# Order of experts, router table, fillers and bias products in a one-core mixture-of-experts step

## What is computed

```python
logits = (x2 @ w_router) + b_router            # 336 x 32
top_v, top_i = lax.top_k(logits, 4)
gates = jax.nn.softmax(top_v, axis=-1)
...
gu = xb @ w_gu[e] + b_gu[e]                    # D_MODEL 1024 -> 2 * D_FF 2048
gate = jnp.minimum(gu[:, :D_FF], 7.0)
up = jnp.clip(gu[:, D_FF:], -7.0, 7.0)
hid = (up + 1.0) * gate * jax.nn.sigmoid(1.702 * gate)
return hid @ w_dn[e] + b_dn[e]                 # 1024 -> 1024
```

## Time and profile before

| what | value |
|---|---|
| median of the runs | 1793.83 us |
| the profiled execution, its own time | 1794.13 us |
| its span | 1792.3 us |
| TensorE (PE) busy | 1596.8 us, 89% |
| VectorE / ScalarE / GpSimd busy | 363.6 / 372.3 / 122.1 us |
| share of the last chain: arrival of gate/up weights | 16% |
| DMA | 477.36 MB, 266 GB/s over the span |
| a free block of the loop: token turn / bias products / hidden turn | 0.71 / 1.09 / 0.66 us |
| the same: one piece of 4 products (8 instructions) | 1.72 us |
| the same: start of the token turn to start of the bias products | 0.94 us |

### The profile page before, as it was taken

One profiled execution on the slowest core, in us unless ns is written; L12 is line 12 of the kernel. 1 busy time (PEld: TensorE's weight loads), 2 busy tenths in 40 slices (PEclk: granted clock), 3 DMA queues, 4 the chain that ended last, 5 costly groups with the idle time before them and its releaser, 6 DMA issues.

```text
span 1792.3 us, 20636 instructions
## 1 busy us (share of the span) xinstructions
PE 1596.8 (89%) x7124; PEld 732.7 (41%) x7125; DVE 363.6 (20%) x859; ACT 372.3 (21%) x724; POOL 122.1 (7%) x219
## 2 busy tenths in 40 slices
PE   6899999999999997988879998878899978899894
PEld 4565665666666643322223332222233322233231
DVE  3443442223231123110101101100111100111015
ACT  3443242353430020110101111101111101111111
POOL 0100000000000000100001010100011100011000
PEclk9989999899999997998989999989899989899997
DMA  7212112221209524899998999999999999849898
GB/s 251 69 47 74 47 48 94 72 71 47 95 1 303 187 99 175 347 409 413 413 405 324 401 354 413 411 409 407 362 363 360 405 409 406 351 179 406 339 403 283
DMA packets 108777, 477.36 MB, mean 266 GB/s; under 512 B 12995, under 2 KB 16944, under 8 KB 75970
## 3 DMA queue, kind: packets, MB, share of 16 engines
q1 hardware_dynamic: 100696, 461.77, 65.9%
q0 software_dynamic: 7808, 15.00, 2.5%
q10 hardware_dynamic: 234, 0.08, 0.0%
HBM read 471.26 MB, written 15.50 MB: 272 GB/s over the span
## 4 chain that ended last, share of the span: by engine, by line
PE 70%; DMA 17%; DVE 5%; issue 3%; SPq 2%; ACT 1%; DVEq 0%; ACTq 0%; POOL 0%; POOLq 0%
PE bank L592 30%; PE bank L975 20%; DMA ring<-in_w_gate_up 16%; PE bank L998 16%; PE bank L596 3%; PE bank L981 1%; DVE r_kv L1346 1%; DVE r_v L1349 1%; DMA b_router_b<-in_b_router 1%; SPq L546 0%; SPq L553 0%; SPq L462 0%; DVE r_c L1349 0%; DVE r_qk L1343 0%; DVE ring L1343 0%
## 5 line engine op out<-in xcount | busy, mean ns | idle before, releaser
L975 PE MATMUL bank<-ring,r_kv 128*64 128x512 f32 x2184 | 521.1, 625 | 95.6 <-DMA ring<-in_w_gate_up 95.6
L975 PEld LDWEIGHTS bank<-ring,r_kv 128*64 128x64 f32 x2184 | 157.1, 142 | 408.7 <-issue 309.0
L998 PE MATMUL bank<-ring,r_kv 128*64 128x512 f32 x1248 | 294.6, 616 | 0.7 <-ACT r_kv L1063 0.7
L592 PE MATMUL bank<-r_xt,ring 128*128 128x336 f32 x848 | 256.6, 458 | 1.8 <-DVE r_xt L1346 1.5
L1343 DVE TENSOR_SCALAR r_kv<-bank 128x512 f32<-128x512 f32 (+1 forms) x80 | 54.9, 687 | 930.5 <-PE bank L981 924.0
L592 PEld LDWEIGHTS bank<-r_xt,ring 128*128 128x128 f32 x848 | 161.7, 194 | 83.4 <-issue 13.2
L998 PEld LDWEIGHTS bank<-ring,r_kv 128*64 128x64 f32 x1248 | 93.8, 145 | 200.6 <-issue 199.7
L1063 ACT ACTIVATE r_xt<-bank 128x512 f32<-128x512 f32 x39 | 23.3, 597 | 521.6 <-PE bank L998 521.6
L592 PE MATMUL bank<-ring 128*128 128x336 f32 (+4 forms) x336 | 98.2, 435 | 4.1 <-DVE ring L1502 3.9
L1289 ACT ACTIVATE r_o<-r_kv 128x512 f32<-128x512 f32 x39 | 24.6, 632 | 324.7 <-DVE r_kv L1343 324.7
L596 PEld LDWEIGHTS bank<-const,r_v 64*128 64x128 f32 (+3 forms) x524 | 45.4, 139 | 79.4 <-DVE r_v L1349 44.5
(11 more groups left out here) (235 smaller groups left out, 988.2 us busy)
## 6 DMA issues: line engine op xcount, KB each, us to landing
ring<-in_w_gate_up SPq DMA_DIRECT2D x256, 1024.0 KB, 17.1
ring<-in_w_down SPq DMA_DIRECT2D x128, 1024.0 KB, 14.6
ring<-in_w_in SPq DMA_DIRECT2D x12, 2048.0 KB, 8.1
ring<-in_w_proj_b SPq DMA_DIRECT2D x2, 2048.0 KB, 8.8
ring<-in_w_proj_a SPq DMA_DIRECT2D x2, 2048.0 KB, 8.9
ring<-in_w_out SPq DMA_DIRECT2D x2, 2048.0 KB, 7.8
ring<-y_rows SPq DMA_DIRECT2D x8, 512.0 KB, 9.1
ring<-in_w_uq SPq DMA_DIRECT2D x2, 1152.0 KB, 9.0
```

The lines of the kernel that those rows point to most:

```text
L592: ins = pe.matmul(out, l, r, start=(n == 0), stop=(n == len(pairs) - 1), **kw)
L975: ins = pe.matmul(half(gate_bank if q < 2 else up_bank, q % 2), xg[:, k, :], w[:, 512 * q:512 * q + 512], start=False, stop=False, skip_gr ...
L998: ins = pe.matmul(half(out_bank, t), hidT[:, j, BLK * h:BLK * h + BLK], w[:, h, 512 * t:512 * t + 512], start=(j == 0 and h == 0), stop=(j ...
```

## The change

- Experts are set apart by rank. VectorE makes for each expert a key (blocks x 32, and the expert's number for ties; expert 0 gets the lowest), its rank by key, and a place for each rank from a table of constants (`rank_at`, the bit-reversed number plus 4; expert 0 stays at place 0). With the counts above the order is 0, 21, 11, 31, **26**, 12, 2, 22, **20**, 16, 6, 27, **10**, 14, 4, 24, 1, 19, 9, 30, **8**, 13, 3, 23, **29**, 17, 7, 28, **18**, 15, 5, 25 (bold: more than one block). Two more products, "ord" and "st", bring blocks and first blocks in that order to all partitions; "pend" goes. SyncE reads the expert of a place from `experti` and loads its weights; `be` holds a block's expert for the biases, `bei` its place.
- One slot table. `spread` has 55 columns in place of 110, the table product writes both halves of the partitions with the same values (24 products of 55 columns), and the token row is worked out from the output row by rounding. GpSimd's part of `spread`, `valc` and "tab2" go.
- Fillers: products of 128x512 that nobody reads, 2 ahead of the turn of tile 2, 2 ahead of "ord", 5 ahead of "tab", 1 ahead of the first turn of tokens.
- Down biases: all 6 products stand within block 0's gate/up pieces, 4 ahead of piece 2 and 2 ahead of piece 5; the loop waits for all six adds.
- In the loop: ScalarE takes the sigmoid straight from the gate bank; VectorE works out min(sigmoid, its value at 7) x (up + 1), then min(gate, 7) x that, the gate read from its bank (the 1 is now added to the up biases once, ahead of the router stage). The two bias products of the up bank stand ahead of the turn of the hidden rows, the two of the gate bank behind it. `down(0)` and `down(1)` stand ahead of `gate_up(0, e1)`.

```diff
+def keep_going(b, n):
+    for _ in range(n):
+        pe.matmul(b[:, :], ident, const[:, 0:512], start=True, stop=True, skip_group_check=True)
...
+            keep_going(begin("x2T", 2, 0), 2)
             x2_turned(2)
...
-            pe.wait_ge(nblkT_set, 1)
-            b = begin("pend")
-            end(group(b[0:NE, 0:1], [(cst("below")[0:NE, 0:NE], nblkT[:, :])]), "pend")
+            keep_going(begin("ord"), 2)
+            pe.wait_ge(order_set, 1)
+            b = begin("ord")
+            end(group(b[:, 0:2 * NE], [(cst("ones")[0:NE, :], ordered[:, :])]), "ord")
+            pe.wait_ge(diag_set, 1)
+            b = begin("st")
+            end(group(b[:, 0:NE], [(cst("ones")[0:NE, :], diag[:, :])]), "st")
+            keep_going(begin("tab"), 5)
...
             for k in range(8):
+                if k == 2:
+                    for n in range(4):
+                        down_bias(banks[4 + n], n // 2, n % 2).then_inc(bd_full, 1)
+                if k == 5:
+                    pe.wait_ge(bd_free, 2)
+                    for n in range(4, 6):
+                        down_bias(banks[n], n // 2, n % 2).then_inc(bd_full, 1)
                 gate_up(k, 0)
...
-                bias(b + 1)
+                bias(b + 1, (2, 3))
                 hidden_turned(b)
-                pe.wait_ge(m_xg, b + 2)
-                gate_up(0, e1)
+                bias(b + 1, (0, 1))
                 pe.wait_ge(m_hidT, b + 1)
                 pe.wait_ge(yrow_free, b + 1)
+                pe.wait_ge(m_xg, b + 2)
                 down(0, e)
                 down(1, e)
+                gate_up(0, e1)
                 down(2, e)
                 gate_up(1, e1)
                 down(3, e)
...
-                act.wait_ge(m_gt, b + 1)
-                act.activation(sg, gt, ACT.Sigmoid, scale=ALPHA).then_inc(m_sig, 1)
+                act.wait_ge(m_gate, b + 1)
+                act.activation(sg, banks[2][:, :], ACT.Sigmoid, scale=ALPHA).then_inc(m_sig, 1)
...
-            signal(dve.tensor_reduce(nblkT, cmp6[0:NE, 0, :], AX.X, ALU.add), nblkT_set, 1)
...
+            step(stt(key, nblk[0:NE, :], float(NE), cst("key", NE)[:, 0:NE], ALU.mult, ALU.add))
+            step(ts(above, key, keyT, ALU.is_gt))
+            step(dve.tensor_reduce(rankT, above, AX.X, ALU.add))
...
+                x = sp.value_load(experti[0:1, bass.ds(e, 1)].bitcast(I32), min_val=0, max_val=NE - 1)
...
-                ts(gt, banks[2][:, :], LIMIT, ALU.min).then_inc(m_gt, 1)
...
-                ts(up, banks[3][:, :], LIMIT, ALU.min, -LIMIT, ALU.max).then_inc(m_read, 1)
+                ts(up, banks[3][:, :], LIMIT + 1.0, ALU.min, 1.0 - LIMIT, ALU.max).then_inc(m_read, 1)
...
-                tt(gt, gt, sg, ALU.mult).then_inc(m_dve, 1)
+                stt(glu, sg, SIG_LIMIT, up, ALU.min, ALU.mult).then_inc(m_dve, 1)
...
-                stt(hid, up, 1.0, gt, ALU.add, ALU.mult).then_inc(m_hid, 1)
+                stt(hid, banks[2][:, :], LIMIT, glu, ALU.min, ALU.mult).then_inc(m_hid, 1)
...
-            pool.tensor_tensor(spread[:, :, 0:NB1], inblk, valc.unsqueeze(2).broadcast_to([128, 12, NB1]), ALU.mult
-                               ).then_inc(tab_p, 1)
```

159 lines of the change are left out of this document (91 added, 68 removed).

## The result

The change takes 1783.98 us (median of 5 runs, 1779.22 to 1789.16), the kernel before 1793.83 us beside it (5 runs, 1791.90 to 1794.33): ratio 0.9948, 95% interval 0.9926 to 0.9971. That is 9.85 us less, where I had forecast 20.6 less. The direction and the range held, the size did not. The profiled execution of the change took 1789.16 us, the slowest of its five, with a span of 1787.3 us where 1792.3 stood; the experiments contain a second execution of the same kernel (a_again) with a span of 1781.7.

A forecast was written before the change was run, and what follows sets the result against it. TensorE was taken as bound by its own work plus 17 stalls on expert weight loads. Loop -15.7, block 1 -1.0, router stage -0.5 and block 0 -3.4 sum to -20.6: 1794.13 becomes 1773.5 us, range 1762 to 1784 (chance 0.72).

The forecast's parts named there:

- The model of the stalls: Loop waits for gate/up weights: from the third transition after a full ring; 96.1 us for 138.0, a gain of 41.9.
- the 17 places named: Expert places forecast to stall in the loop: 3, 4, 7, 8, 11, 12, 15 to 20, 23, 24, 27, 28, 31.
- Spacing alone: Loop: reordering experts by rank, without the other loop changes, was forecast to be worth about 0.
- 24.29: Forecast length in us of a loop block that finds its weights, where 23.60 us stood.
- Two bias products (0.55 us) now fill part of that hole: Behind the hidden rows' turn: a pair costed at 0.55 us in a 0.69 us idle, next product 0.69 us later.
- +26.2 us: Loop: cost of longer free blocks, 38 times 0.69 us, if nothing hid it.
- block 1: Loop's first block: 1.4 us of slow clock goes with the idle ahead of it, forecast -1.0 us.
- second rival: Loop: the clock falls at every turn, each block pays 2.5 to 3 us, about 1807 us; chance 0.05.
- router stage and block 0: Ahead of the loop: forecast -0.5 us for the router stage and -3.4 us for block 0.
- Block 0: First turn to first loop bias: 26.4 us becomes 23.0, -3.4 us (-4.4 to -1.7), with down biases inside the product.
- The stage ahead of it: Router stage: longer table path against earlier token turn and fillers holding the clock; -0.5 us, from -2 to +4.
- the signs I had named: Signs include free blocks 24.3 us, idle about 70 us, first loop bias at 715 to 718, clock above 0.5 from 676 to 690.

The follow-up runs named there:

- e5: The change with all four bias products ahead of the turn again and VectorE's old chain, down pieces still first; run twice, 1782.74 us in one, 0.9939 to 0.9952 of before.
- e8: The change with all four bias products behind the turn of the hidden rows; free block 24.8 us where the clock stays up, kernel time not given in the text.
- e9: The loop with four biases ahead of the turn and down pieces first, keeping only the two fillers before tile 2's turn; within 0.9939 to 0.9952 of before.
- e6: Four biases ahead of the turn, down pieces first, and the next block's token turn moved behind the hidden rows' turn; 0.9994 of before.
- e1: The change with experts left in the order of their numbers; 0.9998 of before.
- e3: The change with the old loop and experts by number, keeping the router table, fillers and down biases; loop 1010.8 us, kernel time not given in the text.
- e2: The change with TensorE's and VectorE's old loop, experts still spaced; loop 1007.5 us, against before slower, if at all, by 0.14%.
- e4: The change without any filler product; 0.9974 of before (0.9956 to 0.9991).
- e7: The change with four of six down bias products replacing the filler ahead of the first token turn; 1785.17 us, 0.9944 of before.
- e10: Token turn behind the hidden rows' turn, with TensorE's wait for turned tokens moved two down pieces later; 0.9942 of before.

## Why the prediction went wrong

**What held.** The model of the stalls: idle times at the 17 places named, ten of them long, and a short idle in the last block. Spacing alone was worth 3 us in the loop, near the 0 of the forecast, but cost 7 us at the end, which the forecast hadn't followed. The measured excess over free blocks is 90.0 us, 6.7 of it in the slow blocks, so 83.3 in stalls, where the forecast had 96.1: the longer free blocks gave the loads more time. The idle time is 56.1 us, where I had named about 70. e5 is the fair test of that model, since its free block (24.4 us) is nearly the one I had costed (24.29): its loop is 15.1 and 15.9 us shorter than before's, where the forecast had 17.4 for 37 blocks, or some 12 if each is 0.14 us longer; and its 93.5 and 92.7 us above 37 free blocks are close to the 96.1.

**The step that failed** is "Two bias products (0.55 us) now fill part of that hole; the next product still starts 0.69 us later than before", and so the term **+26.2 us**. I had halved the 1.09 us of the row of four. But the row itself says that these products have 32 rows each: the four stand in the four groups of rows of the array and run beside each other. The pair takes 1.07 us and outlasts the hole that it was to fill. The pages of both kernels show it in TensorE's busy time for the same number of bias products, before and in the change:

```profile
L965 PE MATMUL bank<-bgu,r_qk 32*64 32x512 f32 x312 | 44.2, 636 | 12.0 <-DVE r_kv L1343 12.0
```

```profile
L983 PE MATMUL bank<-bgu,r_qk 32*64 32x512 f32 x312 | 86.4, 643 | 5.5 <-DVE r_kv L1367 5.3
```

The Trainium skill ("TensorE: Matmul & The Clock Gate", the part on packing small matmuls) states just this, that products in different row groups overlap and together take about as long as one; the traces of the change and of e8 agree (two in 1.07, four in 1.09 us), and I hadn't laid it beside the row. That is 0.17 us of the 0.44 by which a free block is longer than forecast: the down product starts 1.59 us after the turn in the change and 1.42 in e5, with the hole bare. Another 0.14 us is the bare hole itself, 0.83 us later than before in e5 (1.42 for 0.59) and not the 0.69 read off the last block. The last 0.13 us is VectorE: its product now depends on the clip just before it. I had costed that chain at 0 by its durations, which held (0.69 us each, also the one that reads the bank); what I had not costed is the gap between dependent operations, 0.79 against 0.61 us from start to start. The estimated 0.065 us for a PSUM source, from the Trainium skill ("VectorE: DVE Perf Modes", the section on the TRN2 errata), doesn't show in these rows.

In the profiled pair, term by term: 

```
                                       forecast   measured   difference
longer blocks                           +26.2      +43.2      +17.0   (37 x 24.73 - 872.9 = 42.1, and 1.1 behind)
stalls                                  -41.9      -54.7      -12.8   (138.0 to 83.3)
block 1                                  -1.0       -1.4       -0.4
slow blocks with no idle for weights      0         +6.7       +6.7   (second rival, in small)
router stage and block 0                 -3.9       -1.5       +2.4
last reads and stores                     0         +3.4       +3.4
ahead of the router stage                 0         -0.6       -0.6
sum                                     -20.6       -4.9      +15.7
```

Most of the 17.0 came back from the stalls; 4.2 us stay. e5 against a_again shows the same from the other side: 0.30 us less in a free block, 11.1 us in 37, make a loop only 2.6 us shorter (997.2 for 999.8). The slow blocks differ from one execution to the next (6.7 us here, 2.0 in a_again). The runs of the change spread over almost 10 us (1779 to 1789), and this execution is 5.0 us below before's where the median is 9.85 below; how much of that spread is slow blocks, the unprofiled runs don't tell. The execution of a_again, with a span 10.6 us below before's, is nearer the median, and it misses the -20.6 by 10.0: longer blocks less stalls 3.7, the end 3.8, router stage and block 0 2.4, slow blocks 2.0, and -1.9 from block 1 and from ahead of the router stage. So the mis-sized term is the largest, but most of it was paid back; the end, to which the forecast gave nothing, weighs as much in what was left.

**Slow blocks.** The second rival had 0.05 and the right place, "the clock falls at every turn"; in the change it falls at 3 of 22, in e8 at 15 of 27. In e8 the wait ahead of the turn (1.77 us) stands out. In the change the waits are 0.23 and 0.37 us with a pair of biases between and another behind; in e5 they are 0.23, 0.23 and 0.76 us, more in all, and the clock held in all three profiles of that order (e5 twice, e9). It held in e6 too, with 0.87, 0.23 and 0.87 us, more than e8's 1.77 in sum. So the sum of idle time alone doesn't decide; what does, these runs leave open.

**Block 0** was to gain 3.4 us, 1.7 at the least, and gained 0.9 (26.4 to 25.5 us from the first turn to the first loop bias). The down biases went inside the product, as forecast, and the adds beside it. But I had given the clock a middle value, and it was at 0.50 until about 700.7: the last filler ran 2.07 us at half clock, turn and biases took 1.11 and 1.98 us, and the first two pieces 5.5 instead of 3.4. The stage ahead of it gained 0.6 us for -0.5 forecast: the fillers ran at half clock (two for the order product took 3.16 us), the five ahead of the table for all but their last 2 us (7.16 us in all), but these ended at 685.45, 0.8 us behind the table's inputs (684.61), not 2.3. Of the signs I had named, the loop's first bias at 715 to 718 failed (719.25), and the clock above 0.5 between 676 and 690 held for half of it only (0.50 to 683.4, 1.00 from 683.6 to 690.2).

**The end** I hadn't looked at. With the experts spaced, the loads are behind until the last expert: the last block's pieces 6 and 7 come 0.54 and 0.71 us late, SyncE begins to read rows of y back when the weights are barely in, and the last store of y (1762.47) is followed by the last reads 7.9 us later, where 4.9 us stood (1770.41 to 1775.26). Last bias to end is 58.6, 59.5 and 58.5 us with experts by number (before, e1, e3) and 63.1 to 65.5 with experts spaced (the change, a_again, e2, e4, e7, both of e5, e9, e10): it comes with the order. e6 and e8, spaced but with longer blocks, so that the loads lag less, have 61.6 and 60.0. That late loads are what delays the reads is argued from these rows; no run changed the end alone.

**Open:** in the DMA-bound places 16 to 20 the change takes 32.2 us a block on average, where 31.4 stood. The 0.8 us go with the order of the experts and not with the loop: e2 has 32.0 there, e1 31.3 in its stalled runs by number. What they are is not found.

## What to carry to other kernels

Before costing half of a group of products at half its time, look at their rows: products of 32 rows in different groups of the array run beside each other, so a half costs what the whole does, and splitting them over two places pays twice (44.2 us of TensorE in all before, 86.4 in the change). Filling a hole in TensorE's queue helps only if the filler is shorter than the hole; a bare hole of 0.76 us was better than a pair of 1.07. And a reordering that moves slack between loads and compute must be followed to the end of the program, where late loads meet the last stores.

## What the runs showed of the hardware that I had not expected

A pair of 32-row bias products takes 1.07 us, four take 1.09. TensorE's granted clock fell from 1.00 to half in blocks without any wait for DMA: after 1.77 us of waiting on VectorE (15 of 27 times in e8), and in 3 of 22 blocks of the change, whose waits there are 0.23 and 0.37 us. Five fillers of 128x512 in a stage whose clock was at 0.50 took 7.16 us; the clock was 1.00 only for the last 2 us of them and behind them, and at 0.50 again at 690.5, after a wait of 0.39 us and in one of 3.49 us, so nothing was left of it for block 0.
